# A two-layer streaming encoder on one core: two plain gate/up pairs instead of three ahead of the seven-product form, and new orders around it

## The reference

```python
def conv_ffn(x, buf, w_in, conv_w, w_out):
    h = x @ w_in                                   # 1024 -> 2 * 2816
    gate, up = h[..., :D_FF], h[..., D_FF:]
    gate, buf_new = causal_dwconv(gate, conv_w, buf)
    return (jax.nn.silu(gate) * up) @ w_out, buf_new

x = layer_norm(ALPHA * x + y, ln_mix_g[i], ln_mix_b[i])
y, ffb = conv_ffn(x, ff_buf[i], w_ff_in[i], ffconv_w[i], w_ff_out[i])
x = layer_norm(ALPHA * x + y, ln_ff_g[i], ln_ff_b[i])
# odd layer: h = x @ w_in_o (1024 -> 3 * 1024 + 1024 + 16), conv over positions, silu, then DeltaNet
```

## Time and profile before

| what | value |
|---|---|
| median of 3 runs | 3016.79 us (3016.03 to 3018.7) |
| profiled execution, own time | 3017.4 us |
| its span, first to last instruction | 3015.6 us |
| PE busy | 2895.6 us, 96% of the span |
| DVE, POOL, ACT busy | 1841.1, 1443.3, 848.2 us |
| granted TensorE clock, mean | 0.984 |

### The profile page before, as it was taken

One profiled execution on the slowest core, in us unless ns is written; L12 is line 12 of the kernel. 1 busy time (PEld: TensorE's weight loads), 2 busy tenths in 40 slices (PEclk: granted clock), 3 DMA queues, 4 the chain that ended last, 5 costly groups with the idle time before them and its releaser, 6 DMA issues. The chain is left out here.

```text
span 3015.6 us, 55591 instructions
## 1 busy us (share of the span) xinstructions
PE 2895.6 (96%) x23232; PEld 2768.1 (92%) x23232; DVE 1841.1 (61%) x3054; ACT 848.2 (28%) x1570; POOL 1443.3 (48%) x1014
## 2 busy tenths in 40 slices
PE   8999999999999999999999969999999999999996
PEld 7999767899999999998999968887989999999996
DVE  2337675685556566678675646665476555556666
ACT  2212474133333321013321123433132333321012
POOL 2233101247777742226632227887536777763330
PEclk9999999999999999999999989999999999999998
DMA  6120102022222242213322234331412222233221
GB/s 180 44 59 16 50 1 88 8 80 71 73 85 67 87 157 98 87 45 106 105 87 89 80 91 118 86 86 48 134 46 77 76 76 82 73 117 120 95 82 64
DMA packets 278415, 243.81 MB, mean 81 GB/s; under 512 B 51305, under 2 KB 251351, under 8 KB 277655
## 3 DMA queue, kind: packets, MB, share of 16 engines
q1 hardware_dynamic: 278167, 240.26, 25.9%
HBM read 177.32 MB, written 62.91 MB: 80 GB/s over the span
## 5 line engine op out<-in xcount | busy, mean ns | idle before, releaser
L160 PE MATMUL ps<-xhi,whi 128*128 128x364 f32 x2352 | 781.7, 332 | 5.7 <-PEq L922 3.6
L161 PE MATMUL ps<-xlo,whi 128*128 128x364 f32 x2352 | 775.1, 330 | 0.0
L166 PE MATMUL ps<-xhi,wlo 128*128 128x364 f32 x2352 | 774.2, 329 | 0.0
L160 PEld LDWEIGHTS ps<-xhi,whi 128*128 128x128 f32 x2352 | 442.2, 188 | 10.7 <-issue 5.9
L161 PEld LDWEIGHTS ps<-xlo,whi 128*128 128x128 f32 x2352 | 442.4, 188 | 3.2 <-issue 0.3
L166 PEld LDWEIGHTS ps<-xhi,wlo 128*128 128x128 f32 x2352 | 442.0, 188 | 1.4
L1583 POOL TENSOR_SCALAR whi<-wraw 128x1024 fp32r<-128x1024 f32 x88 | 111.7, 1269 | 588.4 <-PE ps L166 529.0
L1850 PE MATMUL ps<-xlo,whi 128*128 128x272 f32 (+1 forms) x1216 | 352.1, 290 | 0.0
L1849 PE MATMUL ps<-xhi,whi 128*128 128x272 f32 (+1 forms) x1216 | 351.3, 289 | 0.0
L1851 PE MATMUL ps<-xhi,wlo 128*128 128x272 f32 (+1 forms) x1216 | 351.0, 289 | 0.0
L2358 DVE TENSOR_TENSOR z<-ps,z 128x364 f32<-128x364 f32 x384 | 202.8, 535 | 144.7 <-PE ps L166 144.7
(11 more groups left out here) (511 smaller groups left out, 6622.1 us busy)
## 6 DMA issues: line engine op xcount, KB each, us to landing
wraw<-in_w_ff_in SPq DMA_DIRECT2D x88, 512.0 KB, 4.8
wraw<-in_w_ff_out SPq DMA_DIRECT2D x44, 512.0 KB, 4.0
qkvz<-eo_ob SPq DMA_DIRECT2D x32, 546.0 KB, 4.6
wraw<-in_w_in_o SPq DMA_DIRECT2D x32, 512.0 KB, 4.5
xlo<-hidden SPq DMA_DIRECT2D x28, 546.0 KB, 4.7
hidden<-eo_ups SPq DMA_DIRECT2D x18, 546.0 KB, 2.7
hidden<-oo_ups SPq DMA_DIRECT2D x18, 546.0 KB, 2.8
z<-residual SPq DMA_DIRECT2D x6, 1456.0 KB, 9.5
```

Of the source, the lines that this page charges most:

```text
L160: one = pe.matmul(out, whi, xhi, start=start, stop=False)
L161: two = pe.matmul(out, whi, xlo, start=False, stop=False)
L166: return pe.matmul(out, wlo, xhi, start=False, stop=stop)
```

## The change

PLAIN goes from 3 to 2, so each layer has 20 seven-product pairs instead of 19. Around it:

* S2 is the first of the seven products instead of A11, and ACT prepares its operand first.
* DVE makes the low halves of t1 and t2 ahead of the second pair's convolution; that of t3 comes after its last tap, ahead of `silu`.
* On ACT, four weight operands of the first seven-product pair now stand behind the sigmoid of the last plain pair; before, two did.
* `square_sums` stands one step earlier in the mix stage.
* In the out stage, DVE's `sums` are spread in threes between the last pair's steps, and one store stands behind the loads of the first hidden units.
* In the odd stage five units instead of four are run split by split (HEAD), the first mean stands behind two products instead of one, and ACT copies three products ahead of `root(4)` instead of one. ACT's own order of the copies stays (`kept_place`).

```diff
@@ layer_block
-    PLAIN = 3
+    PLAIN = 2
+    HEAD = 5
@@ slot
         if kind in ("odd", "out"):
-            return (t + 1) % 4
+            return (t + 2) % 4
-    A11, S2, S3, S1, A12, S4, A22 = range(OPS)
-    BANK = (0, 1, 3, 2, 0, 2, 3)
+    S2, A11, S3, S1, A12, S4, A22 = range(OPS)
+    BANK = (1, 0, 3, 2, 0, 2, 3)
@@ operand
-            k = slice((n + 4) % 8 * BLOCK, ((n + 4) % 8 + 1) * BLOCK)
+            k = slice(n % 8 * BLOCK, (n % 8 + 1) * BLOCK)
@@ odd_place (kept_place is what it was)
-            return 4 * q + i if i < 4 else 4 * SPL + SPL * (i - 4) + q
+            return HEAD * q + i if i < HEAD else HEAD * SPL + SPL * (i - HEAD) + q
@@ SP, out units
-                    if t < 2:
-                        store_hidden(FT - 3 + t)
+                    if t == 0:
+                        store_hidden(FT - 3)
...
+                    if t == 2:
+                        store_hidden(FT - 2)
@@ POOL, out units
-                        pool.wait_ge(s("prod"), products(NPR - 1, 1, (S2, S1, S4, A22)[t]))
+                        pool.wait_ge(s("prod"), products(NPR - 1, 1, (S2, S3, A12, A22)[t]))
@@ PE, odd stage
                 odd_product(0, 0)
+                odd_product(1, 0)
                 mean(5)
-                odd_product(1, 0)
+                odd_product(2, 0)
                 variance(4)
-                odd_product(2, 0)
                 odd_product(3, 0)
+                odd_product(4, 0)
                 odd_product(0, 1)
                 odd_product(1, 1)
                 variance(5)
-                odd_product(2, 1)
-                odd_product(3, 1)
-                for i in range(4):
+                for i in range(2, HEAD):
+                    odd_product(i, 1)
+                for i in range(HEAD):
                     odd_product(i, 2)
@@ ACT, ahead of the first seven-product pair
             gates_kept(1)
+            difference_high(2)
+            operand_high(0, S2)
+            operand_high(0, A11)
             sigmoid_of(1)
-            difference_high(2)
-            gates_kept(2)
-            operand_high(0, A11)
-            operand_high(0, S2)
-            operand_high(0, S3)
-            operand_high(0, S1)
-            sigmoid_of(2)
-            operand_high(0, A12)
-            operand_high(0, S4)
+            for j in (S3, S1, A12, S4):
+                operand_high(0, j)
             last_difference_high()
@@ ACT, odd stage
-                kept(0, 0)
+                for i in range(3):
+                    kept(i, 0)
                 root(4)
-                kept(1, 0)
...
-                kept(2, 0)
@@ DVE, mix stage
-                    if q >= 1 and j == 2:
+                    if q >= 1 and j == 1:
                         square_sums(q - 1)
@@ DVE, plain pairs
                 if t == 0:
                     difference(0)
+                else:
+                    difference_low(2)
                 silu(t)
-                if t == 1:
+                gated(t)
+                if t == 0:
+                    for n in range(1, 4):
+                        difference(n)
                     difference_low(0)
                     difference_low(1)
-                gated(t)
-                if t == 0:
-                    difference(1)
-                    difference(2)
-                    difference(3)
-                if t == 1:
-                    difference_low(2)
             difference_low(3)
@@ DVE, start of the out stage
-            sums(0)
-            sums(1)
+            for seq in range(0, 3):
+                sums(seq)
             tap(t, 1)
-            sums(2)
+            for seq in range(3, 6):
+                sums(seq)
             tap(t, 2)
-            sums(3)
-            sums(4)
+            for seq in range(6, 9):
+                sums(seq)
             silu(t)
-            sums(5)
+            for seq in range(9, 12):
+                sums(seq)
             gated_up(NPR - 1)
```

More of the change, by code:

```diff
@@ L1404, in odd_group, with kept_place @@
             return (i + 1) % 2, i // 2
+        def kept_place(i, q):
+            return 4 * q + i if i < 4 else 4 * SPL + SPL * (i - 4) + q
         def odd_place(i, q):
-            return 4 * q + i if i < 4 else 4 * SPL + SPL * (i - 4) + q
+            return HEAD * q + i if i < HEAD else HEAD * SPL + SPL * (i - HEAD) + q
         def odd_column(i):
@@ L1786, in _ @@
             MOVING = [
-                ((m.xhi, m.xlo), 0, 0), ((t2hi, t2lo), 0, None), ((t3hi, t3lo), 0, None), ((t1hi, t1lo), 0, None),
+                ((t2hi, t2lo), 0, None), ((m.xhi, m.xlo), 0, 0), ((t3hi, t3lo), 0, None), ((t1hi, t1lo), 0, None),
                 ((m.xhi, m.xlo), HQ, 0), ((m.xhi, m.xlo), HQ, 1), ((t4hi, t4lo), 0, None)]
@@ L1838, in block_product @@
                 if i == 0 and e == 0 and j in (S1, S2, S3):
-                    pe.wait_ge(s("t_lo"), {S2: 1, S3: 2, S1: 3}[j])
+                    pe.wait_ge(s("t_lo"), {S1: 1, S2: 2, S3: 3}[j])
                 if i == 0 and e == 0 and j == A22:
@@ L1902, in odd_product @@
                 else:
-                    pe.wait_ge(s("odd_free"), odd_place(i - 2, q) + 1)
+                    pe.wait_ge(s("odd_free"), kept_place(i - 2, q) + 1)
                 for k in range(KD):
@@ L1989, in _ @@
                 variance(5)
-                odd_product(2, 1)
-                odd_product(3, 1)
-                for i in range(4):
+                for i in range(2, HEAD):
+                    odd_product(i, 1)
+                for i in range(HEAD):
                     odd_product(i, 2)
-                for i in range(4, NODD):
+                for i in range(HEAD, NODD):
                     for q in range(SPL):
@@ L2073, in sigmoid @@
                 if k == 3:
-                    act.wait_ge(s("odd_free"), odd_place(i, SPL - 1) + 1)
+                    act.wait_ge(s("odd_free"), kept_place(i, SPL - 1) + 1)
                 act.activation(sg[:, :], (gb[:, 0:TW] if k == 3 else cv[:, :]), ACT.Sigmoid).then_inc(s("sig_odd"), 1)
@@ L2189, in _ @@
                 if more:
-                    operand_high(i + 1, A11)
+                    operand_high(i + 1, S2)
                 first_kept(i, 1)
                 if more:
-                    for j in (S2, S3, S1, A12):
+                    for j in (A11, S3, S1, A12):
                         operand_high(i + 1, j)
@@ L2531, in _ @@
             convolve(t)
-            sums(0)
-            sums(1)
+            for seq in range(0, 3):
+                sums(seq)
             tap(t, 1)
-            sums(2)
+            for seq in range(3, 6):
+                sums(seq)
             tap(t, 2)
-            sums(3)
-            sums(4)
+            for seq in range(6, 9):
+                sums(seq)
             silu(t)
-            sums(5)
+            for seq in range(9, 12):
+                sums(seq)
             gated_up(NPR - 1)
-            for seq in range(6, DONE):
+            for seq in range(12, DONE):
                 if seq % CHUNK in (12, 13):
@@ L2614, in conv_odd @@
                 x = raw[:, k, :]
-                dve.wait_ge(s("odd_free"), odd_place(i, SPL - 1) + 1)
+                dve.wait_ge(s("odd_free"), kept_place(i, SPL - 1) + 1)
                 for r in range(3):
```

## The result

The changed kernel takes 3033.13 us (median of 4 runs, 3032.3 to 3034.38), beside 3017.74 us (3016.03 to 3018.76) for the kernel before on the same chip. The ratio is 1.0052, with a 95% interval of 1.0039 to 1.0064: slower, by 15.4 us of medians, where 11.7 were forecast. The profiled span is 3030.5 us instead of 3015.6.

The account below looks back on a forecast made before the run. PE, busy 96% of the span, was taken as the bound. Terms -11.4, -5.4, +19.4, -5.4 and +14.5 sum to +11.7, from 3017.4 to 3029.1, forecast as median 3028.5 us; range 3015 to 3039.

Parts of the forecast that it names:

- Rival 3: Odd stage loses more: PE's unit 6 needs ACT's copy of unit 4; 4 us more, 3032.5 us, chance 14%.
- Part 1: Square sums one step earlier: second variance starts 3.7 us sooner, 2.0 of slow clock saved; 5.7 us a layer, -11.4.
- Parts 2 and 3: 2: plain pair replaced by seven-product pair, -5.4 us; 3: hand-over to seven-product form covered by two plain pairs, +19.4 us.
- S: Cost of the hand-over to the seven-product form in each layer, forecast 9.7 us, bounds 3.8 to 11.7.
- the lock's charge: In the hand-over, DVE and POOL SBUF steps exclude each other, so they alternate at 2.42 and 1.30 us each.
- Rivals 1 and 2: 1: no lock in hand-over, 3.8 us a layer, 3016.7 us, 15%; 2: hand-over covered, 3009.1 us, 8%.
- Part 4: Start of the out stage: earlier loads and split, sums in threes; 3.4 us less in first layer, 2.0 in second, -5.4.
- some short waits go: Out stage, sums in threes: the 1.57 us and short waits go, 2.4 us in first layer, 1.0 in second.
- the clock may hold: Start of the out stage: DVE's second low half ends some 0.5 us earlier, clock may stay up; 1.0 us a layer.
- Part 5: Odd stage: PE waits 15 us for POOL's split of unit 4, then 2.5 for ACT's copy of unit 2; +14.5 us.
- the 4.30 us and its slow clock go: Odd stage: PE's 4.30 us wait ahead of the mean vanishes, as 4.0 us more work stands before it.

Follow-up runs that it names:

- experiment 5: The kernel before with only the square sums one step earlier, in both layers: 3003.54 us, ratio 0.9953.
- experiment 3: The changed kernel without POOL's weight sums and low halves in each layer's first seven-product pair: 3015.0 us, ratio 0.9989 to the kernel before.
- experiments 6 and 10: 6: the kernel before with only the out stage's edits, 3014.86 us; 10: the changed kernel run again, nothing else changed, 3032.47 us.
- Experiment 2: The changed kernel with POOL's split of odd unit 4 ahead of residual(3) and residual(4): 3016.12 us, ratio 0.9998 to the kernel before.
- experiment 7: The kernel before with the odd stage's first mean behind two products and ACT's three copies ahead of root(4), HEAD at 4: 3018.02 us, ratio 1.0000.
- experiments 9 and 11: 9: the kernel before with 53 or 256 idle instructions more on PE, 3021.28 and 3017.41 us; 11: the changed kernel with 203 more, 3027.59 us.

## Why the prediction was right, and where it was not

The sign and the range held, and so did the mechanisms that were priced, but for a part of the out stage. 3033.13 lies in the range of 3015 to 3039, 4.6 us above the number. That it is so near is partly luck: the delta stage's 6.6 us, which the forecast did not have, stand against 2.6 of chance in the front and 0.8 in the forecast terms. Rival 3's time, 3032.5, is nearer still, but its mechanism is not there: the odd stage lost 15.0 us, not 18.5.

**Part 1, right.** Waits of 1.54 us and no slow clock, 5.8 and 6.5 us for the 5.7 forecast; alone it gives 13.9 by medians (experiment 5). On the clock of the old trace `variance` starts at 588.2 (585.63 and the 2.58 of the earlier front), forecast 588.5.

**Parts 2 and 3, right, S a little too large.** The plain pair took 23.95 us and a seven-product pair 21.31 before and 21.33 now. (The forecast's 21.23 divides a window that ends at 1090 us, but that stage's last matmul starts at 1091.4.) So the pair itself gives 2.6 us and not 2.7. The first seven-product pair took 29.8 us, 8.5 over the steady ones: S is 8.5, not 9.7. The steady pairs' 0.02 us each are the other 0.4. PE's two pairs end 8.4 us earlier than on the old clock: DVE's low t2 ended there at 659.6 (forecast 660.0), `silu` at 669.7 (670.8), and S3 started at 670.4 (671.5). The waits are 4.5, 0.6 and 1.4 us, with about 2 us of slow clock behind the first.

The term that was mis-sized is the lock's charge: 2.42 + 1.30 = 3.72 us a round, where the rows show 3.4, so DVE lost 1.0 for each POOL step of 1.30. Three rounds account for some 0.4 of the 1.1 us by which S3 came earlier than forecast. Most of the rest lies in the second convolution and its taps, where POOL's two low halves cost DVE 1.4 us (0.79 became 1.33 and 2.75 became 3.66) and some 2.0 had been charged.

The Trainium skill ("SBUF — State Buffer", "SBUF: two separate sides") says that the port pair is an exclusive lock for the whole instruction, and that PE and ACT never wait on it. The stretched steps and experiment 3 agree with the kind of effect, and ACT's casts of 2.02 and 0.61 us stayed as they were. The 0.3 us less a round do not speak against it: an engine's records overlap. Unstretched, DVE starts two low halves 2.34 us apart (646.57 and 648.91 in experiment 3) and POOL two of its steps 1.25 (685.97 and 687.22 in the kernel before), which adds up to 3.59; the last 0.15 is open.

Rivals 1 and 2 are out: with POOL's steps there S is 8.5, and with them gone the cover is complete. How far it would be covered without a lock, but with POOL's steps in the chain, no run shows.

**Part 4, smaller.** 3.1 and 1.1 us for 3.4 and 2.0, and alone 2.6 by medians. The step that failed is that "some short waits go", with its 1.0 us for the second layer: there the waits for DVE's `sums` did not go but grew from one of 0.80 us to three of 0.73, 0.49 and 0.39. In the first layer they went. The slow clock at the start of the stage, which the forecast left as it was but for "the clock may hold", comes in some executions only (experiments 6 and 10).

**Part 5, right.** 14.4 us of PE waiting for POOL's split of unit 4, 2.2 us for ACT's copy of unit 2, 15.0 in all for 14.5. Experiment 2 shows that it was this wait: with the split ahead 13.6 us of the stage come back. The forecast's "the 4.30 us and its slow clock go" is true of the place and worth nothing: experiment 7 removes that wait alone and the time stays, since PE meets the same DVE chain at product (0, 1) and the slow clock behind it. The sum did not suffer, because it was taken at the last `variance`, behind the long wait.

**What no step held: the delta stage.** The forecast took a stage with unchanged code to keep its time. It became 6.6 us longer, and 5.2 of them are idle times of PE that the profile puts down to issue. The changed kernel's PE issues 53 instructions more by then (23453 instead of 23400 in the traces). The page of the changed kernel's profile has instruction blocks among the DMA queues:

```profile
q8 instruction: 185, 3.03, 0.4%
```

3.03 MB in 185 packets are 16.4 KB each, and PE's 47588 recorded instructions fill 186 blocks of 256, so this queue brings PE's. Shifting the stream by 53 brings the idle times, by 256 does not, and completing the change's 53 to 256 takes them away again with 8 us (experiments 9 and 11). With all 43 idle times at one place in the block of 256 and 1.2 to 1.6 us behind a packet, it is shown that PE waits there for its instructions, and that the place of this stage's matmuls in the stream decides where. How much the stage loses varies at one and the same place, from 336.5 to 342.2 us.

The Trainium skill ("Runtime: NRT & Kernel Launch", "Instruction fetch mechanics") says that blocks are of 256 instructions and 16 KiB and that crossing a border is mostly hidden. The size of the blocks agrees with packets and experiments; here the fetch is hidden beside matmuls of 272 to 364 columns (no idle time put down to issue in the seven-product stage) and not beside matmuls of 64.

The longest idle time grows from 1.05 us with the shift alone to 2.15 and more in the changed kernel because the block comes later. In the seven traces with 53 its packet starts 2.8 to 3.2 us after PE's previous border where the idle time is 0.78 to 1.33, and 3.9 to 4.4 us after it where it is 2.15 to 2.70. Why it starts later stays open: the DMA engines were busy for 0.81 to 0.86 of that time in the first three traces and for 0.91 to 0.96 in the other four, and no run varies their load alone.

The 2.6 us in the front are chance: the same kernel gave 1.3 us of them back.

## What to carry to other kernels

Before units are reordered on the busiest engine, look up where the engine that prepares each of them has it in its own list: here one product pulled ahead of 16 small steps of POOL cost 15 us, and with the split moved ahead too the stage lost 1.5. A wait on the busy engine is worth removing only if its releaser is not on a chain that the next wait ends; experiment 7 is how to find out. When a stage with untouched code changes its time and the engine's idle time is put down to issue, compare how many instructions stand ahead of it and whether the idle times lie a whole number of blocks apart, and try a padding of the missing number up to a block before looking for a cause in the stage.

## What the runs showed that I had not expected

* The place in the instruction stream is worth up to 8 us in this kernel, 0.25%: 342.1 and 334.1 us for the same stage of matmuls of 64 columns. Every idle time over 0.6 us that the profile puts down to issue there was at a block border and ended 1.2 to 1.6 us after a block had come.
* Where DVE and POOL alternate, a round is shorter than the sum of the durations of their steps: 3.4 us for 2.42 and 1.30.
* An idle time of 2.4 us of PE at the start of the out stage brought a stretch at half clock of 3.6 us in one execution and none in another, and one of 1.83 us in the same code did so too. The same code gave an out stage that differed by some 4 us between profiles. The single idle times of 1.5 us ahead of `variance` were never followed by a slow clock, but six idle times of 0.2 to 0.9 us in 7 us were (experiment 7).
* Between profiles of the same code the large stages of long matmuls agree to 0.2 us. What varies is the front (550.3 to 553.7) and the start of the out stages, so a comparison stage by stage finds differences that medians with a spread of 5 us do not.
